# A mixture-of-experts block on one core: more expert tiles at both ends of the gate stage, and all first one-hots made on ScalarE

## Chip, core and metric

The kernel runs on one core of a Trainium2 chip. The metric is the device time of one execution in microseconds, the median of several runs.

## What is computed

One layer for a prompt of 512 tokens and 32 sample tokens (8 sequences of 4): two kinds of attention, an output projection, and then the part that matters here, a PEER layer (128 x 128 experts of one neuron each, 8 retrieval heads, the best 16 each), with a last normalization behind it. For a block of tokens `xt` of 1024 values:

```python
q = (xt @ w_query).reshape(T, 8, 256)
s1 = einsum("thc,nc->thn", q[..., :128], k1)
s2 = einsum("thc,nc->thn", q[..., 128:], k2)
v1, i1 = top_k(s1, 16); v2, i2 = top_k(s2, 16)
cand = v1[..., :, None] + v2[..., None, :]
cidx = i1[..., :, None] * 128 + i2[..., None, :]
top, pos = top_k(cand.reshape(T, 8, 256), 16)
eidx = take_along_axis(cidx.reshape(T, 8, 256), pos, -1)
g = softmax(top)
hid = einsum("thkd,td->thk", u_tab[eidx], xt)
out = einsum("thk,thkd->td", g * gelu(hid), v_tab[eidx])
```

All data is float32.

## The kernel before

The 512 + 32 tokens lie in five token tiles. Tiles 1 to 3 (384 prompt tokens) are computed densely: all 16,384 experts in 128 expert tiles of 128, with a matrix of gates that is zero where an expert was not chosen. Tile 0 and the sample tokens go sparsely: for each of the 128 slots of a token the row of the table is gathered from memory (32 rounds of five gathers, each of 128 rows of 1024) and VectorE forms the dot product.

Float32 products are made of three passes over split operands: the rounded high part (`uhi`, `vhi`, made by ScalarE) and the rest (`ulo`, `vlo`, made by GpSimd in the query stage and by VectorE later). The stages that matter:

- **Query stage** (`@block` functions from L1382). In a loop of eight turns: a head's queries and scores, VectorE's top-16 selection, and four expert tiles of hidden values, `hidden_product` (L1322, 24 matmuls of 384 columns). ScalarE makes a tile's Gelu and issues its store to memory (`hidden_gelu`, L1333), then rounds the tile after the next (`u_split_hi`, L1313). Behind the loop `QX` = 8 more expert tiles run (L1510, L1476, L1433) while VectorE ends the last head and the softmax of the gates, with ScalarE's Exp at the last of them (L1478). The SP queue loads tiles four ahead, and then spreads the sample's indices and gates (L1399 to L1406).
- **Gate stage** (L1677 to L1898). Each stage's block ends with a barrier of all engines. Three transposes (L1679) bring the indices and gates of a token into columns (`slotT`). Then six turns, each of `GTI` = 14 expert tiles interleaved with 16 groups of four tokens. For a group, four products of one-hot matrices (`oh` for the first index, `og` for the second, weighted by the gate) give the gates of four tokens over all experts in PSUM. ScalarE evicts them into `gst` (L1862), and after eight groups issues a store of 2 MB (`gate_matrix`, L1853). VectorE makes the low part of every tile (L1785), `og` of every group, `oh` of every second one by a comparison with a row of numbers (L1762, L1763), and the dots of the sparse tokens (L1772). ScalarE makes the other `oh` as four Abs of a difference and one Relu (`first_one_hot`, L1830). Four one-hot buffers stand in a ring, and they are made two groups ahead. POOL issues the gathers and cuts `slotT` into chunks of 32 tokens. Behind the turns `GX` = 4 expert tiles run, then ten dots, the Gelu of the sparse hidden values (L1879), and `coef`.
- **Value stage** (L1903 on). For each of the 128 expert tiles VectorE weighs the hidden values with the gates (`af`, L2001), ScalarE rounds `vhi` and `ahi`, VectorE makes `vlo` and `alo`, and 18 matmuls of 512 columns accumulate into PSUM. VectorE also adds the gathered value rows (L1978). SP loads value tiles one at a time, and hidden values and gates four tiles at a time (`load_gates`, L1625) into two buffers.

The order is written by hand. In a turn ScalarE does a tile's part behind every second half of a tile (L1845) and a group's part behind the half where TensorE does the group:

```python
for i in range(GTI):
    for part in range(2):
        half_tile(i, part)
        upto = N2 * (2 * i + part + 1) // (2 * GTI)
        while at < upto:
            group(at)
            at += 1
```

## Time and profile before

| | us |
|---|---|
| median of 3 runs (lowest to highest) | 1867.72 (1864.65 to 1868.74) |
| profiled execution, own time | 1864.95 |
| its span, first to last instruction | 1863.4 |
| TensorE matmuls busy | 1691.0 (91%) |
| VectorE busy | 1397.9 (75%) |
| ScalarE busy | 776.9 (42%) |
| GpSimd busy | 570.6 (31%) |
| mean transfer rate | 253 GB/s |

PE is TensorE (PEld its weight loads), DVE VectorE, ACT ScalarE, POOL GpSimd, SP the engine that only issues transfers. A busy share is an average over stages with different limits; what a stage could give is read from the waits in it. A time in brackets in a timeline is the engine's idle time before the instruction, with who ended it. Matmuls are pipelined, so their durations overlap: what one costs is read from start to start.

### The profile page before, as it was taken

To read this page: it belongs to the slowest core of one execution; us is meant where nothing else is said; L and a number is where in the kernel's file an instruction comes from. 1 tells how busy PE (TensorE), PEld (TensorE's weight loads), DVE (VectorE), ACT (ScalarE), POOL (GpSimd) and SP (SyncE) were. 2 spreads that over 40 slices of the span, in tenths; PEclk is the share of its full clock that TensorE was granted. 3 is DMA by queue.
4 is the path that set the end of the run, shared out by engine and by line. 5 is a ranking of instruction groups with operands and counts; after the bars stand their busy time and mean duration, and the time that the engine had idled before them with its cause. 6 is when DMAs were issued, how large, how long until landed. Compare 5 with 4: busy or idle time off the path is not lost. (4 is left out here: it accounts for less than half of the span.)

```text
span 1863.4 us, 30406 instructions
## 1 busy us (share of the span) xinstructions
PE 1691.0 (91%) x9914; PEld 1486.2 (80%) x9914; DVE 1397.9 (75%) x3179; ACT 776.9 (42%) x1195; POOL 570.6 (31%) x508
## 2 busy tenths in 40 slices
PE   5997898779799999779989999996899999999994
PEld 4997643449699999779989999996688888888883
DVE  3234267534389999968979888987898999999995
ACT  3222034221444433256657666663333333333333
POOL 0010280000354544433323333332433333333330
PEclk9998899899799999989999999998899999999997
DMA  3242361261343432379998998999999999999992
GB/s 112 97 174 94 121 214 46 83 232 43 116 143 111 138 115 82 124 259 350 345 376 304 366 354 332 380 338 361 363 386 387 384 384 384 384 384 389 385 385 81
DMA packets 195215, 470.82 MB, mean 253 GB/s; under 512 B 17922, under 2 KB 100482, under 8 KB 192558
## 3 DMA queue, kind: packets, MB, share of 16 engines
q1 hardware_dynamic: 124014, 240.30, 36.7%
q0 software_dynamic: 50944, 178.96, 26.0%
q10 hardware_dynamic: 20160, 50.34, 6.9%
q8 instruction: 52, 0.85, 0.2%
q14 instruction: 45, 0.37, 0.1%
HBM read 411.97 MB, written 61.32 MB: 254 GB/s over the span
## 5 line engine op out<-in xcount | busy, mean ns | idle before, releaser
L226 PE MATMUL hp<-mid_hi,uhi 128*128 128x384 f32 x1024 | 355.3, 347 | 12.0 <-issue 6.0
L227 PE MATMUL hp<-mid_lo,uhi 128*128 128x384 f32 x1024 | 345.7, 338 | 0.0
L228 PE MATMUL hp<-mid_hi,ulo 128*128 128x384 f32 x1024 | 344.4, 336 | 0.0
L226 PE MATMUL va<-vhi,ahi 128*128 128x512 f32 x768 | 299.6, 390 | 22.6 <-DVE alo L2010 22.6
L227 PE MATMUL va<-vlo,ahi 128*128 128x512 f32 x768 | 299.4, 390 | 0.0
L228 PE MATMUL va<-vhi,alo 128*128 128x512 f32 x768 | 299.2, 390 | 0.0
L2026 POOL DMA_INDIRECT gathered<-in_v_experts,idx_row x160 | 186.5, 1166 | 323.9 <-DVEq L1981 289.7
L1719 POOL DMA_INDIRECT gathered<-in_u_rows,idx_row x160 | 169.2, 1058 | 312.9 <-DVE hrow L1772 228.0
L226 PEld LDWEIGHTS hp<-mid_hi,uhi 128*128 128x128 f32 x1024 | 193.8, 189 | 17.3 <-DVE ulo L1785 8.6
L1316 ACT ACTIVATE uhi<-uw 128x1024 fp32r<-128x1024 f32 x128 | 135.7, 1060 | 151.9 <-PE hp L228 101.9
L1955 ACT ACTIVATE vhi<-vw 128x1024 fp32r<-128x1024 f32 x128 | 134.8, 1053 | 144.3 <-DMA vw<-in_v_experts 144.1
L228 PEld LDWEIGHTS hp<-mid_hi,ulo 128*128 128x128 f32 x1024 | 193.6, 189 | 0.0
L227 PEld LDWEIGHTS hp<-mid_lo,uhi 128*128 128x128 f32 x1024 | 193.6, 189 | 0.0
L226 PEld LDWEIGHTS va<-vhi,ahi 128*128 128x128 f32 x768 | 144.5, 188 | 53.0 <-issue 22.9
L1772 DVE CUSTOM_DVE_ANT_0 gathered<-gathered,x2p 128x1024 f32<-128x1024 f32 x150 | 178.7, 1213 | 8.7 <-DMA gathered<-in_u_rows,idx_row 6.4
L228 PEld LDWEIGHTS va<-vhi,alo 128*128 128x128 f32 x768 | 144.6, 188 | 30.1
L227 PEld LDWEIGHTS va<-vlo,ahi 128*128 128x128 f32 x768 | 144.6, 188 | 30.0
L2005 DVE TENSOR_TENSOR vlo<-vw,vhi 128x1024 fp32r<-128x1024 f32 x128 | 156.1, 1219 | 14.6 <-ACT vhi L1955 14.3
L1978 DVE SCALAR_TENSOR_TENSOR acc<-gathered,crow,acc 128x1024 f32<-128x1024 f32 x128 | 164.0, 1282 | 3.7 <-DMA gathered<-in_v_experts,idx_row 3.7
L1320 POOL TENSOR_TENSOR ulo<-uw,uhi 128x1024 fp32r<-128x1024 f32 x42 | 106.2, 2529 | 130.5 <-ACT uhi L1316 130.4
L1785 DVE TENSOR_TENSOR ulo<-uw,uhi 128x1024 fp32r<-128x1024 f32 x86 | 105.1, 1222 | 54.1 <-ACT uhi L1316 53.4
L1957 ACT ACTIVATE ahi<-af 128x384 fp32r<-128x384 f32 x128 | 66.9, 522 | 184.6 <-DVE af L2001 184.5
(328 smaller groups left out, 3306.2 us busy)
## 6 DMA issues: line engine op xcount, KB each, us to landing
uw<-in_u_experts SPq DMA_DIRECT2D x128, 512.0 KB, 6.7
vw<-in_v_experts SPq DMA_DIRECT2D x128, 512.0 KB, 10.6
hidden_values<-gelu_out ACTq DMA_DIRECT2D x128, 192.0 KB, 5.4
gate_matrix<-gst ACTq DMA_DIRECT2D x12, 2048.0 KB, 12.7
mid_hi<-hidden_values SPq DMA_DIRECT2D x32, 768.0 KB, 11.9
mid_lo<-gate_matrix SPq DMA_DIRECT2D x32, 768.0 KB, 16.6
pw<-in_w_qk SPq DMA_DIRECT2D x16, 512.0 KB, 3.5
qw<-in_w_query SPq DMA_DIRECT2D x16, 512.0 KB, 5.0
```

What stands on the lines that cost most here:

```text
L226: nc.tensor.matmul(out, a_hi, b_hi, start=first, stop=False)
L227: nc.tensor.matmul(out, a_hi, b_lo, start=False, stop=False)
L228: return nc.tensor.matmul(out, a_lo, b_hi, start=False, stop=last)
L1316: nc.scalar.activation(uhi[:, i], uw[:, r], ACT.Copy).then_inc(u_hi, 1)
L1320: nc.gpsimd.tensor_tensor(ulo[:, i], uw[:, r], uhi[:, i].bitcast(F32), ALU.subtract).then_inc(u_lo, 1)
L1719: nc.gpsimd.indirect_dma_start(gb[:, b], None, u_table, bass.IndirectOffsetOnAxis(ap=idx_row[:, slot, b:b + 1], axis=0)).then_inc(gathered ...
L1772: nc.vector.tensor_tensor_reduce(out=gb[:, b], in0=gb[:, b], in1=x2p[:, b // SG], scale=1.0, scalar=0.0, op0=ALU.mult, op1=ALU.add, accum_ ...
L1785: nc.vector.tensor_tensor(ulo[:, i], uw[:, r], uhi[:, i].bitcast(F32), ALU.subtract).then_inc(u_lo, 1)
L1955: nc.scalar.activation(vhi[:, c], vw[:, c], ACT.Copy).then_inc(s["vhi"], 1)
L1978: nc.vector.scalar_tensor_tensor(acc0[:], gb[:, c], crow[:, q, c:c + 1], acc0[:], ALU.mult, ALU.add).then_inc(s["s0"], 1)
L2005: nc.vector.tensor_tensor(vlo[:, c], vw[:, c], vhi[:, c].bitcast(F32), ALU.subtract).then_inc(s["vlo"], 1)
L2026: nc.gpsimd.indirect_dma_start(gb[:, b], None, v_table, bass.IndirectOffsetOnAxis(ap=idx_row[:, slot, b:b + 1], axis=0)).then_inc(gathered ...
```

## The change

`QX` goes from 8 to 16 and `GX` from 4 to 8, so `GTI` falls from 14 to 12. What stood at the start of the gate stage moves into the query stage's last tiles: the transposes and their copies behind tiles 12 to 14, the copy of `x2p` to PSUM at tiles 0 and 1, VectorE's building of the tables, and the first round of gathers on POOL. Exp stands at tile 11. On the SP queue the loads of tiles 15 to 19 go behind the transfers of the gates. What stood at the start of the value stage moves to the last eight tiles of the gate stage: the first four value tiles are rounded and split, the first round of value rows is gathered, the first gates are loaded and the first four tiles weighed. The ten last dots are dealt out between the low parts. Gates are weighed in place (`hd`, no `af`), so a buffer of `load_gates` is free only when `alo` is made. The second pair of buffers lies where the expert tiles lay (`uw`). ScalarE makes `oh` for all groups.

```diff
-        QX, GX = 8, 4
+        QX, GX = 16, 8
+        MIX = 11
...
-                for e in range(QX + UR):
+                for e in range(MIX + UR):
...
+                for e in range(MIX + UR, QX + UR):
+                    u_fetch(sp, RT * NH + e, e % UR)
...
+                    if e == QX - 3:
+                        for b in range(3):
+                            fetch_u_row(pool, 0, 0, b)
...
+                    if e == QX - 2:
+                        for b in range(3, ROW):
+                            fetch_u_row(pool, 0, 0, b)
...
+                    hidden_gelu(act, RT * NH + e, e % 2)
+                    if e < 2:
+                        act.wait_ge(s["sev"], 2 * NH + 1)
+                        act.wait_ge(x2r_spread, 16 * SG)
+                        nc.scalar.activation(x2p[:, e], x2r[:, e], ACT.Copy).then_inc(gs["x2p"], 1)
+                    if e == MIX:
                         act.wait_ge(s["exin"], 1)
                         nc.scalar.activation(GG[:], GG[:], ACT.Exp).then_inc(s["ex"], 1)
-                    hidden_gelu(act, RT * NH + e, e % 2)
+                    if MIX < e <= MIX + 3:
+                        act.wait_ge(gs["tr"], e - MIX)
+                        nc.scalar.activation(slotT[:, e - MIX - 1], tp, ACT.Copy).then_inc(gs["trev"], 1)
...
+                    if MIX < e <= MIX + 3:
+                        i = e - MIX - 1
+                        pe.wait_ge(s["ev"], 2 * NH + 1)
+                        pe.wait_ge(table_prep, (2, 2, 3)[i])
+                        if i:
+                            pe.wait_ge(gs["trev"], i)
+                        for t in range(TDT):
+                            last = nc.tensor.transpose(tp[:, t * P:(t + 1) * P], (I1, I2, GG)[i][:, t + 1], ident[:])
+                        last.then_inc(gs["tr"], 1)
...
+                dve.wait_ge(table_prep, 3)
+                nc.vector.tensor_copy(sgate[:, :, 0:SG], GG[:, 0].rearrange("p (g k) -> p g k", k=SG))
+                dve.wait_ge(table_spread, 16 * 2 * SG)
+                nc.vector.tensor_copy(sgate[:, :, SG:], spread_gate[:])
+                nc.vector.tensor_copy(eidx[:, 0:SR, SG:], spread_idx[:]).then_inc(gs["tab"], 1)
+                dve.wait_ge(gs["tab"], 1)
+                nc.vector.tensor_copy(idx_row[:], eidx[:, 0:RJ]).then_inc(gs["idx"], RJ)
+                dve.sem_inc(gs["dot"], ROW)
...
+        def weigh(dve, c, par):
+            nc.vector.tensor_tensor(hd[par][:, c].rearrange("p (c t) -> p c t", c=NCH),
+                                    hd[par][:, c].rearrange("p (c t) -> p c t", c=NCH), gt[par][:, :, c], ALU.mult).then_inc(xs["a"], 1)
+
+        def round_v(act, c):
+            nc.scalar.activation(vhi[:, c], vw[:, c], ACT.Copy).then_inc(xs["vhi"], 1)
+
+        def rest_of_v(dve, m, c):
+            dve.wait_ge(xs["vhi"], m + 1)
+            nc.vector.tensor_tensor(vlo[:, c], vw[:, c], vhi[:, c].bitcast(F32), ALU.subtract).then_inc(xs["vlo"], 1)
+
+        def round_a(act, m, c, par):
+            act.wait_ge(xs["a"], m + 1)
+            nc.scalar.activation(ahi[:, c], hd[par][:, c], ACT.Copy).then_inc(xs["ahi"], 1)
+
+        def rest_of_a(dve, m, c, par):
+            dve.wait_ge(xs["ahi"], m + 1)
+            nc.vector.tensor_tensor(alo[:, c], hd[par][:, c], ahi[:, c].bitcast(F32), ALU.subtract).then_inc(xs["alo"], 1)
...
                         pe.wait_ge(s["oh"], j * N2 + i + 1)
-                        if i % 2:
-                            pe.wait_ge(s["first"], j * N2 // 2 + i // 2 + 1 + GR // 2)
+                        pe.wait_ge(s["first"], j * N2 + i + 1 + GR)
                         pe.wait_ge(s["ev"], j * N2 + i + 1)
...
-                for b in range(ROW):
-                    fetch_row(0, 0, b)
                 over_turns(pool, turn)
                 for b in range(ROW):
-                    fetch_row(SR - 1, 1, b)
+                    fetch_u_row(pool, SR - 1, 1, b)
+                for b in range(ROW):
+                    fetch_v_row(pool, 0, 0, b)
...
-                        if i % 2 == 0:
-                            nc.vector.tensor_scalar(oh[:, i % RING, k], iota[:], col(1), None, ALU.is_equal)
                         last = nc.vector.tensor_scalar(og[:, i % RING, k], iota[:], col(0), col(2), ALU.is_equal, ALU.mult)
...
+                last_dots = [(q, b) for q in range(2) for b in range(ROW)]
                 for e in range(GX - 2):
                     split_lo(NK - GX + e + 2, e % 2, (e + 2) % UR)
-                for q in range(2):
-                    for b in range(ROW):
+                    for q, b in last_dots[3 * e:3 * e + 3]:
                         dve.wait_ge(gathered[b], 16 * (SR - 2 + q) + 16)
                         nc.vector.tensor_tensor_reduce(out=gb[:, b], in0=gb[:, b], in1=x2p[:, b // SG], scale=1.0, scalar=0.0,
                                                        op0=ALU.mult, op1=ALU.add,
                                                        accum_out=hid[:, SR - 2 + q, b:b + 1]).then_inc(s["dot"], 1)
+                    if e == GX - 4:
+                        dve.wait_ge(s["dot"], SR * ROW + ROW)
+                        nc.vector.tensor_copy(idx_row[:, 0:BR], eidx[:, 0:BR]).then_inc(xs["idx"], BR)
+                        dve.sem_inc(xs["fetched"], ROW)
+                        dve.wait_ge(stored[1], 16 * (NI + 1))
+                        for c in range(GT):
+                            rest_of_v(dve, c, c)
                 dve.wait_ge(s["act"], 1)
                 nc.vector.tensor_tensor(coef[:], hid[:], sgate[:], ALU.mult)
+                dve.wait_ge(gld[0], 32)
+                for c in range(GT):
+                    weigh(dve, c, 0)
+                for c in range(GT):
+                    rest_of_a(dve, c, c, 0)
...
-                        if i % 2 and i + 2 < N2:
+                        if i + 2 < N2:
                             first_one_hot(j, i + 2)
-                        elif i % 2 and not last:
+                        elif not last:
                             first_one_hot(j + 1, i + 2 - N2)
...
+                    if 1 <= e <= GT:
+                        act.wait_ge(stored[0], 16 * (NI + 1))
+                        act.wait_ge(vld[e - 1], 16)
+                        round_v(act, e - 1)
+                    if e == GX - 3:
+                        act.wait_ge(s["dot"], SR * ROW + ROW)
+                        act.wait_ge(s["hrow"], NI)
+                        nc.scalar.activation(hid[:], hid[:], ACT.Gelu).then_inc(s["act"], 1)
+                    if e == GX - 2:
+                        act.wait_ge(s["mm"], NI * N2 + RING)
+                        for c in range(GT):
+                            round_a(act, c, c, 0)
...
+                for e in range(UR, GX):
+                    u_fetch(sp, NK - GX + e, e % UR)
                 for u in range(2):
                     sp.wait_ge(stored[u], 16 * (NI + 1))
                 for i in range(2):
                     sp.wait_ge(ge_stored[i], 8 * 2 * GT + 16)
-                sp.wait_ge(h_mm, NK + 2)
-                for g in range(2):
-                    load_gates(sp, g, g)
-        pick.close()
-        query.close()
+                sp.wait_ge(s["cut"], 2 * NI)
+                load_gates(sp, 0, 0)
+                for i in range(GT):
+                    sp.wait_ge(xs["vlo"], i + 1)
+                    sp.dma_start(vw[:, i], A["v_experts"][GT + i]).then_inc(vld[i], 16)
+                sp.wait_ge(u_lo, NK + 2)
+                load_gates(sp, 1, 1)
...
-                            sp.wait_ge(s["a"], (g - 1) * GT)
+                            sp.wait_ge(s["alo"], (g - 1) * GT)
```

POOL, at the end of the query stage and the start of the gate stage, before (`ulo` is the low part of an expert tile, `gathered` the buffer of gathered rows):

```order
L1320 TENSOR_TENSOR ulo<-uw,uhi 128x1024 x12
L1350 UNCONDITIONAL_BRANCH
L1702 UNCONDITIONAL_BRANCH
L1711 COPY chunkT<-slotT 128x96
L1719 DMA gathered<-in_u_rows,idx_row 128x1024 x5
```

and now:

```order
L1324 TENSOR_TENSOR ulo<-uw,uhi 128x1024 x18
L1369 DMA gathered<-in_u_rows,idx_row 128x1024 x3
L1324 TENSOR_TENSOR ulo<-uw,uhi 128x1024
L1369 DMA gathered<-in_u_rows,idx_row 128x1024 x2
L1324 TENSOR_TENSOR ulo<-uw,uhi 128x1024
L1372 UNCONDITIONAL_BRANCH
L1786 UNCONDITIONAL_BRANCH
L1795 COPY chunkT<-slotT 128x96
```

The five gathers of the first round stand ahead of the last two low parts and of the end of the block (the two branches).

ScalarE inside a turn, before (`gst` the evicted gates, `oh` the first one-hots, `uhi` the rounded tile):

```order
L1840 ACTIVATE oh<-oh 128x512
L1334 REGISTER_ALU
L1335 ISA
L1336 ACTIVATE gelu_out<-hp 128x384
L1338 ISA
L1338 DMA hidden_values<-gelu_out 128x384
L1314 ISA
L1316 ACTIVATE uhi<-uw 128x1024
L1861 REGISTER_ALU
L1862 ACTIVATE gst<-ggp 128x4x128
L1334 REGISTER_ALU
L1336 ACTIVATE gelu_out<-hp 128x384
```

and now:

```order
L1911 ACTIVATE oh<-oh 128x512
L1338 REGISTER_ALU
L1339 ISA
L1340 ACTIVATE gelu_out<-hp 128x384
L1342 ISA
L1342 DMA hidden_values<-gelu_out 128x384
L1318 ISA
L1320 ACTIVATE uhi<-uw 128x1024
L1933 REGISTER_ALU
L1934 ACTIVATE gst<-ggp 128x4x128
L1907 ACTIVATE oh<-iota,chunkT 128x128 x4
L1911 ACTIVATE oh<-oh 128x512
```

Every `gst` is now followed by four Abs and a Relu on `oh`; before, every second one.

ScalarE in a turn now, from the issue of a gate store on:

```order
L1925 DMA gate_matrix<-gst 128x4096
L1933 REGISTER_ALU
L1934 ACTIVATE gst<-ggp 128x4x128
L1907 ACTIVATE oh<-iota,chunkT 128x128 x4
L1911 ACTIVATE oh<-oh 128x512
L1338 REGISTER_ALU
L1340 ACTIVATE gelu_out<-hp 128x384
L1342 ISA
L1342 DMA hidden_values<-gelu_out 128x384
L1320 ACTIVATE uhi<-uw 128x1024
```

One group (eviction and one-hots) follows the store, then a tile with its own hidden store. Behind these rows stand a group, a tile, a group, and then the Gelu that writes the buffer this hidden store reads; at a turn's end it is the same with a tile first.

## Rows read from the trace of the kernel before

**Rows 1.** Stages: us; busy of PE, PEld, DVE, ACT, POOL; clock; DMA share; GB/s

```profile
746.70:780.00 33.30, 32.65 (x187) 32.01 (x185) 30.69 (x104) 10.70 (x16) 20.53 (x8) 1.00 0.47 172
780.00:806.60 26.60, 2.36 (x10) 1.59 (x10) 17.82 (x68) 5.83 (x7) 2.34 (x1) 0.58 0.12 42
806.60:1273.90 467.30, 448.28 (x2787) 438.13 (x2785) 407.33 (x986) 310.21 (x506) 164.56 (x163) 0.99 0.94 351
1273.90:1290.80 16.90, 16.87 (x99) 16.55 (x97) 12.60 (x22) 4.88 (x7) 6.37 (x7) 1.00 0.95 346
1290.80:1313.30 22.50, 0.00 (x0) 0.00 (x0) 12.25 (x20) 4.30 (x6) 8.04 (x9) 0.55 1.03 339
1313.30:1837.50 524.20, 524.15 (x2304) 433.55 (x2304) 474.29 (x579) 191.28 (x254) 181.69 (x155) 1.00 1.02 371
```

**Rows 2.** Groups by line, the six gate turns: count | busy, mean ns | idle before, releasers

```profile
L226 PE MATMUL hp<-mid_hi,uhi 128*128 128x384 f32 x673 | 236.5, 351 | 11.4 <-issue 6.0 <-DVE ulo L1785 5.2
...
L1785 DVE TENSOR_TENSOR ulo<-uw,uhi 128x1024 fp32r<-128x1024 f32 x83 | 101.4, 1222 | 49.9 <-ACT uhi L1316 49.2 <-DVE hid L1780 0.2
...
L1836 ACT ACTIVATE oh<-iota,chunkT 128x128 f32<-128x128 f32 x192 | 59.6, 388 | 0.0
...
L1336 ACT ACTIVATE gelu_out<-hp 128x384 f32<-128x384 f32 x84 | 40.8, 486 | 89.9 <-PE hp L228 61.2 <-DMA hidden_values<-gelu_out 28.4
L1840 ACT ACTIVATE oh<-oh 128x512 f32<-128x512 f32 x48 | 30.4, 633 | 1.5
```

**Rows 3.** Timeline of PE: start, us; one group of the gate stage

```profile
1263.68 1.05 PE L1693 MATMUL ggp<-og,oh 128*128 128x128 f32 x8
1264.49 0.42 PE L226 MATMUL hp<-mid_hi,uhi 128*128 128x384 f32 x1
```

**Rows 4.** Timeline of PE at seam 1: first transposes, first product

```profile
803.08 0.87 PE L1683 MATMUL ggp<-ident,I 128*128 128x128 f32 x3 [23.11 <-PEq L1350]
...
806.58 0.67 PE L226 MATMUL hp<-mid_hi,uhi 128*128 128x384 f32 x1
```

**Rows 5.** Timeline at seam 1: ACT, SP's queue, POOL

```profile
797.03 0.74 ACT L1480 ACTIVATE GG<-GG 128x640 f32<-128x640 f32 x1 [14.60 <-DVE GG L1600]
...
799.94 2.45 SPq L1406 DMA_DIRECT2D spread_gate<-GG  x4
...
781.20 2.34 POOL L1320 TENSOR_TENSOR ulo<-uw,uhi 128x1024 fp32r<-128x1024 f32 x1 [1.68 <-ACT uhi L1316]
...
811.07 0.95 POOL L1719 DMA_INDIRECT gathered<-in_u_rows,idx_row  x1 [0.30 <-issue]
```

**Rows 6.** The page's DMA issues: count, KB each, us to landing

```profile
uw<-in_u_experts SPq DMA_DIRECT2D x128, 512.0 KB, 6.7
...
hidden_values<-gelu_out ACTq DMA_DIRECT2D x128, 192.0 KB, 5.4
...
mid_lo<-gate_matrix SPq DMA_DIRECT2D x32, 768.0 KB, 16.6
```

**Rows 7.** Timeline of ACT, one stretch of a turn without a free moment

```profile
873.55 1.14 ACT L1862 ACTIVATE gst<-ggp 128x512 f32<-128x512 f32 x1
874.48 1.24 ACT L1836 ACTIVATE oh<-iota,chunkT 128x128 f32<-128x128 f32 x4
...
876.28 0.47 ACT L1336 ACTIVATE gelu_out<-hp 128x384 f32<-128x384 f32 x1
...
878.32 1.11 ACT L1862 ACTIVATE gst<-ggp 128x512 f32<-128x512 f32 x1
```

**Rows 8.** Timeline of ACT: two gate stores and the Gelu held by a store

```profile
855.32 0.71 ACTq L1853 DMA_DIRECT2D gate_matrix<-gst  x1
...
871.50 0.49 ACT L1336 ACTIVATE gelu_out<-hp 128x384 f32<-128x384 f32 x1 [2.37 <-DMA hidden_values<-gelu_out]
...
884.95 0.34 ACTq L1853 DMA_DIRECT2D gate_matrix<-gst  x1
...
900.12 0.49 ACT L1336 ACTIVATE gelu_out<-hp 128x384 f32<-128x384 f32 x1 [3.10 <-DMA hidden_values<-gelu_out]
```

185 lines of the change are left out of this document (85 added, 100 removed).

## Prediction

> **What bounds the kernel now.** I read first the busy times stage by stage, then who made TensorE wait, then the in-order work of each engine that feeds it. In the stage table [rows 1] TensorE works through the eight expert tiles at the end of the query stage in 33.3 us, 4.16 us a tile. Then come 26.6 us with almost nothing on it, 467.3 us of six gate turns, four more tiles in 16.9 us, 22.5 us with nothing, and the value stage: 524.2 us, TensorE busy in all of it. So the value stage can give nothing, and the change can only win in the two holes (49 us together) and in the turns.
>
> A turn lasts 467.3 / 6 = 77.9 us. TensorE needs 14 tiles of 4.16 us and 16 groups of one-hot products. A group takes 1264.49 - 1263.68 = 0.81 us [rows 3], so a turn's own work is 58.2 + 13.0 = 71.2 us, and 6.7 us a turn are waits and slower work. One wait is 6.0 us that nothing in the profile explains and 5.2 us wait on VectorE's low parts [rows 2]; the hidden product starts late, once at the loop's return, else by parts of a us. The turns are thus bound by TensorE, with VectorE close behind it.
>
> **Seam 1, query to gate.** Removed: the hole of 26.6 us. In it run the softmax tail, the table's transfers, the three transposes and the start of the gathers. Added before the barrier:
> - eight tiles moved here, 8 x 4.16 = +33.3 us;
> - three sets of transposes between tiles, each 0.87 us [rows 4] at the half clock that the hole leaves (0.58 in its mean, [rows 1]), 0.5 at full clock: +1.5 us;
> - a late tile. The SP queue now loads tile 15 of the seam only behind the transfers of the gates. Exp ran at 797.03 [rows 5]; now it stands on ScalarE behind the rounding and Gelu of tile 11, whose product ends at 746.7 + 12 x 4.16 = 796.6, and so ends near 800.6, 2.8 us later than 797.77. The gate transfers, issued from 799.94 for 2.45 us [rows 5], move to about 802.7 to 805.2. The tile is issued at 805.2, just when ScalarE wants to round it. Loads take 6.7 us at the median [rows 6]; half the engines' time is free here, so I take 4. Rounding, about 1 us, the greater part of ScalarE's 2.04 for a tile [rows 7], and the low part on GpSimd, 2.34 [rows 5], end near 813, and TensorE wants the tile at 810.7: +2.3 us;
> - the end of the block. GpSimd does the last low part, but two row gathers stand ahead of it, 0.95 + 0.30 = 1.25 us each [rows 5]; three others stand before the low part of the tile ahead. Counted along its queue, 3 gathers, a low part, 2 gathers and the last low part end about 7.3 us behind the last product. The barrier takes 0.7: the SP queue had ended at 799.94 + 2.45 = 802.39 [rows 5] and TensorE began at 803.08 [rows 4]. TensorE stands 8.0 us. Bounds: 4.2 (rounding, low part and barrier alone) and 11.
>
> Sum 45.1 us for 26.6: **+18.5 us**. Exp, the building of the tables, the x2p and slotT copies lie beside the products: ScalarE is taken for 2.04 us [rows 7] of each 4.16. If that cover goes, they cost their 3 to 4 us.
>
> **The turns.** Each turn loses 2 tiles and keeps its 16 groups: TensorE needs 12 x 4.16 + 13.0 = 62.9 us. VectorE drops two low parts and all 32 one-hot comparisons of a turn. ScalarE takes them: every group now has four Abs and a Relu where every second one had. The order is one queue, so its costs are start-to-start times [rows 7]: an eviction 874.48 - 873.55 = 0.93, a one-hot set 876.28 - 874.48 = 1.80, a tile (Gelu, its store's issue, the rounding) 878.32 - 876.28 = 2.04 us. Before: 14 x 2.04 + 16 x 0.93 + 8 x 1.80 = 57.8 us. Now: 12 x 2.04 + 16 x 0.93 + 16 x 1.80 = **68.2 us**. ScalarE becomes the longest queue, 5 us above TensorE.
>
> To this comes a wait of ScalarE itself. Twice a turn a 2 MB gate store is issued on its DMA queue, and a hidden store behind it lands late: the Gelu that reuses its buffer began 871.50 - 855.32 = 16.2 and 900.12 - 884.95 = 15.2 us after such a gate store [rows 8], having waited 2.37 and 3.10 us; in all 28.4 us of the turns go there [rows 2]. Until now ScalarE had time to spare, so nothing was lost. In the new order (third excerpt of the order, and the same at a turn's end) ScalarE needs 12.2 us of its own from the gate store to the Gelu that waits: three groups and two tiles (12.2). It will stand there 15.7 - 12.2 = 3.5 us, twice: +7.0. A turn is then **75.2 us**.
>
> Six turns are 451.2. The last gate store's wait falls behind the turns, -3.5; filling and draining the queue at both ends, -3.0 (less than two one-hot sets); the 6.0 us of TensorE at the loop's return stay, but that turn's store wait hides in it, +2.5. So 447.2 instead of 467.3: **-20.1 us**.
>
> Other bounds of a turn: at 351 GB/s and 0.94 of the DMA engines [rows 1] a turn moved 27.3 MB. Less two tiles and their stores (0.72 MB each) it is 25.9 MB, and with the engines always busy (373 GB/s) 69.5 us. So a turn lies between 69.5 and, with half of before's 6.7 us of loss on top of 75.2, about 78.4.
>
> The Trainium skill (ScalarE: Activation LUTs, Rules for kernel authors) says to use VectorE and not ScalarE for relu and the like, and to budget some 0.3 us for each ACTIVATE plus 0.83 ns an element. By that a one-hot set would be 2.4 us, 9 us more a turn, and the sum would end slower by about 50 us. The trace has 1.80 us start to start, and that decides.
>
> **Seam 2, gate to value.** Before: 16.9 + 22.5 = 39.4 us. Now eight tiles, 33.3 us. The last dots, the fifth row's gather, the first four value tiles' high and low parts and the first gates lie beside them. VectorE has 6 low parts, 10 dots and 4 value low parts for it, 20 of 1.22 us [rows 2] or a little less, and 8 short ones: under 29 us. What stays is the end: Gelu and issue of the last hidden store, 1.0 us, its landing, 5.4 us at the median [rows 6], for which ScalarE waits before the barrier, 0.7 for the barrier, and 0.9 for a low part late behind a dot that waits for its gather: 8.0 us (bounds 4 and 12). 41.3 for 39.4: **+1.9 us**.
>
> **Value stage.** TensorE needs its 524.2 us and has its first four tiles ready: 0. The gates are now weighed in place, so their buffer is free some 3 us later, after the low part of the group before; they took 16.6 us to land [rows 6], in a cycle of 16.4 us a group. The lead of a group with which the stage starts covers that.
>
> **Sum.** +18.5 - 20.1 + 1.9 = +0.3 us on the profiled execution's 1864.95, so 1865.3. The median of the runs lies 2.8 us above that execution; that gives 1868.1, and I forecast **1868 us**. What a measurement can tell from no change is 0.2%, 3.7 us.
>
> **Rivals.**
> (a) *TensorE stays the bound.* The waits on stores shrink because the DMA engines have fewer tiles a turn, and ScalarE catches up. For it: ScalarE's 68.2 us is only 5 above TensorE's. A turn keeps today's 6.7 us of loss: 62.9 + 6.7 = 69.6, six are 417.6, -49.7; with both seams -29.3: 1838 us on the runs' scale. Against it: the order shows no free stretch on ScalarE for a wait of 3 us.
> (b) *Slower: ScalarE's lag reaches TensorE.* The low part of tile m+2 needs ScalarE's rounding, which waits in line behind one-hot sets; TensorE has one tile and one or two groups, 5 to 6 us, until it needs it, and 2.04 + 1.22 us of that are spent. Once ScalarE lags over 2 us, both stall in turn. At 3.2 us a turn, the upper bound of 78.4, it is +19: 1887 us. For it: VectorE's low parts already cost TensorE 5.2 us [rows 2].
> (c) *Slower: gates land late in the value stage.* It decides if landing passes 17 us. At 18 us each of 15 pairs of groups takes 1.6 us more, 24 us, less the lead of 16: +8, 1876 us.
> (d) *Short activations do not overlap.* 4 x 0.388 + 0.633 [rows 2] = 2.19 us a set, 6.2 us a turn, +37: 1905. [...]
> (e) *The change doesn't do what it says*: a barrier or the late tile keeps the holes as long as they were, so 33.3 + 1.5 us are added at seam 1, not 18.5: 1884 us.
>
> **Numbers.** Forecast case, a turn of 73.5 to 76.5 us: 0.53, which alone spans 1857 to 1876; (a) and what lies between 0.24; (b) 0.12; (c) 0.05; (d) 0.02; (e) 0.04. Half of the bounds' width at the seams is in the first case, so 0.17 of it is faster by over 0.2%, 0.20 within, 0.16 slower. Faster 0.41, same 0.20, slower 0.39. The range takes half of (a) and of (b): 1842 to 1886.
>
> **What would show it.** Seam 1: TensorE stands 6 to 10 us at the barrier, and one low part late near the 15th tile. The turns: gate stores of a turn's end 75 us apart; on ScalarE almost no wait for TensorE (61.2 us now [rows 2]) but still some 35 us for hidden stores; TensorE's waits are for ScalarE's one-hots, a releaser that is missing now. Seam 2: about 7 us between last hidden and first value product. Wrong it would be if turns are under 72 us with ScalarE idle for TensorE, or if value products wait for low parts in mid stage.

## The result, and the profile after

The changed kernel takes 1903.88 us at the median of four runs (1902.51 to 1907.4), the kernel before 1868.23 on the same chip (1864.65 to 1873.72). The ratio is 1.0197, its 95% interval 1.018 to 1.0214: **slower by 1.8 to 2.1%**, 36 us. The forecast was 1868, its range 1842 to 1886. The profiled execution took 1902.88 us, its span is 1901.3. In the experiments below, one execution of seam2_order ran at a lower clock, 1998.87 us, and its median leaves it out.

First the stages of the changed kernel, in the columns and with the cuts of [rows 1]: seam 1 behind the eighth tile, the turns, the products of seam 2, the wait at its end, the value stage, the end.

```profile
785.40:838.10 52.70, 38.30 (x202) 36.80 (x200) 26.19 (x68) 17.60 (x24) 27.72 (x15) 0.89 0.48 164
838.10:1296.40 458.30, 408.28 (x2497) 399.42 (x2498) 356.27 (x782) 362.63 (x719) 152.66 (x157) 0.96 0.92 336
1296.40:1340.40 44.00, 37.54 (x192) 36.29 (x191) 32.56 (x51) 16.80 (x23) 17.25 (x15) 0.91 0.90 334
1340.40:1350.40 10.00, 0.03 (x1) 0.00 (x0) 0.00 (x0) 0.62 (x2) 0.15 (x1) 0.75 1.06 386
1350.40:1874.70 524.30, 524.26 (x2302) 433.90 (x2303) 472.04 (x572) 194.72 (x250) 182.70 (x156) 0.99 1.00 366
```

Seam 1 took 52.7 us where 26.6 stood, the turns 458.3 where 467.3 stood, seam 2 54.0 (44.0 and 10.0) where 39.4 stood; the value stage did not change. Neither TensorE (408 us busy of 458) nor ScalarE (363) fills the turns now. And 5.4 us were lost before any of it, in code that the change does not touch; the last copy of scores began at 737.52 us before and at 742.95 after.

From that copy on every profile below is cut into the same pieces: to the first hidden product of the turns (seam 1), to the last eviction of a gate group (turns), to the first value product (seam 2), to the end. The prediction in this scale: 42.5 us from the copy to the eighth tile's end at 780.0 before, and 45.1 behind it.

| | ahead | seam 1 | turns | seam 2 | value on | span |
|---|---|---|---|---|---|---|
| before | 737.5 | 69.1 | 467.6 | 39.2 | 550.1 | 1863.4 |
| predicted | 737.5 | 87.6 | 447.2 | 41.3 | 550.1 | 1863.7 |
| after | 742.9 | 95.4 | 458.1 | 54.0 | 550.9 | 1901.3 |
| difference to the prediction | +5.4 | +7.8 | +10.9 | +12.7 | +0.8 | +37.6 |

**The turns.** The groups of instructions there, in the columns of [rows 2]:

```profile
L226 PE MATMUL hp<-mid_hi,uhi 128*128 128x384 f32 x577 | 207.3, 359 | 16.5 <-PEq L1372 9.1 <-issue 5.1 <-DVE ulo L1850 2.3
...
L1907 ACT ACTIVATE oh<-iota,chunkT 128x128 f32<-128x128 f32 x384 | 119.0, 387 | 7.5 <-POOL chunkT L1795 7.5
...
L1777 PE MATMUL ggp<-og,oh 128*128 128x128 f32 x768 | 107.2, 284 | 42.3 <-DVE og L1828 42.3
...
L1340 ACT ACTIVATE gelu_out<-hp 128x384 f32<-128x384 f32 x72 | 34.6, 481 | 48.3 <-PE hp L228 27.5 <-DMA hidden_values<-gelu_out 20.8
```

TensorE now waits 42.3 us ahead of the one-hot products, and the releaser named is VectorE's second one-hots. In the kernel before this was 7.3 us (columns: us in total, times, longest):

```profile
PE ggp L1693 <- DVE og L1763: 7.3, 13, 1.2
```

ScalarE's queue is fuller than its busy time of 363 us says: 42 us of its idle time (37.1 and 5.0 in the waits) lie between Gelu and rounding, where it issues the store, so about 405 us are its own work. One of TensorE's waits, in time (start, us, engine, line), ScalarE first, then VectorE, then TensorE:

```profile
850.20 1.12 ACT L1934 ACTIVATE gst<-ggp 128x512 f32<-128x512 f32 x1
851.09 1.24 ACT L1907 ACTIVATE oh<-iota,chunkT 128x128 f32<-128x128 f32 x4
852.37 0.63 ACT L1911 ACTIVATE oh<-oh 128x512 f32<-128x512 f32 x1
852.90 0.47 ACT L1340 ACTIVATE gelu_out<-hp 128x384 f32<-128x384 f32 x1
...
854.00 1.06 ACT L1320 ACTIVATE uhi<-uw 128x1024 fp32r<-128x1024 f32 x1 [0.62 <-ACT gelu_out L1340]
...
855.09 1.23 DVE L1850 TENSOR_TENSOR ulo<-uw,uhi 128x1024 fp32r<-128x1024 f32 x1 [2.93 <-ACT uhi L1320]
856.24 1.11 DVE L1828 TENSOR_SCALAR og<-iota,chunkT 128x128 f32<-128x128 f32 x4
...
857.59 1.13 PE L1777 MATMUL ggp<-og,oh 128*128 128x128 f32 x8 [1.33 <-DVE og L1828]
```

The tile was finished near 851.0, half way between two groups of TensorE. ScalarE was then in an eviction and a set of one-hots, until 852.90; Gelu, the store's issue and the rounding took until 855.0. VectorE had stood 2.93 us for the rounding with its own one-hots in line behind the low part, and TensorE, 1.33 us early, waited for them. Every second group had such a set before; now every group has one.

**Seam 1.** First VectorE's softmax tail in the kernel before:

```profile
790.77 1.83 DVE L1585 TENSOR_TENSOR eq<-eq,XF 128x1280 bf16<-128x1280 bf16 x2
...
794.82 0.32 DVE L1590 TENSOR_TENSOR pk<-eq 128x160 f32<-128x160 bf16 x1
...
799.09 0.82 DVE L1612 TENSOR_TENSOR GG<-GG,sm 128x640 f32<-128x640 f32 x1
```

and in the changed kernel VectorE's tail, GpSimd, Exp and the late tile on ScalarE, SP's queue, TensorE:

```profile
796.36 6.00 DVE L1636 TENSOR_TENSOR eq<-eq,XF 128x1280 bf16<-128x1280 bf16 x2
...
804.59 2.30 DVE L1641 TENSOR_TENSOR pk<-eq 128x160 f32<-128x160 bf16 x1
...
810.84 2.75 DVE L1663 TENSOR_TENSOR GG<-GG,sm 128x640 f32<-128x640 f32 x1
...
799.13 2.42 POOL L1324 TENSOR_TENSOR ulo<-uw,uhi 128x1024 fp32r<-128x1024 f32 x1 [0.66 <-ACT uhi L1320]
...
830.90 0.95 POOL L1369 DMA_INDIRECT gathered<-in_u_rows,idx_row  x1 [0.30 <-issue]
831.87 2.35 POOL L1324 TENSOR_TENSOR ulo<-uw,uhi 128x1024 fp32r<-128x1024 f32 x1
...
808.78 0.74 ACT L1520 ACTIVATE GG<-GG 128x640 f32<-128x640 f32 x1 [2.61 <-DVE GG L1651]
...
819.81 1.06 ACT L1320 ACTIVATE uhi<-uw 128x1024 fp32r<-128x1024 f32 x1 [6.64 <-DMA uw<-in_u_experts]
...
816.07 2.00 SPq L1315 DMA_DIRECT2D uw<-in_u_experts  x4
...
809.28 0.61 PE L1561 MATMUL ggp<-ident,I 128*128 128x128 f32 x3 [2.17 <-DVE sample_idx L1656]
...
822.30 0.52 PE L1561 MATMUL ggp<-ident,GG 128*128 128x128 f32 x3 [2.26 <-ACT slotT L1523]
823.35 0.69 PE L226 MATMUL hp<-mid_hi,uhi 128*128 128x384 f32 x1 [0.53 <-POOL ulo L1324]
838.36 0.68 PE L226 MATMUL hp<-mid_hi,uhi 128*128 128x384 f32 x1 [9.07 <-PEq L1372]
```

The two products of ranks and indices took 6.00 us where they took 1.83 before, the sum behind them 2.30 for 0.32, the gates' last product 2.75 for 0.82. Exp came 65.8 us behind the last copy of scores (59.5 before), and all that follows with it: the loads behind the gates' transfers were issued at 816.07 and ScalarE stood 6.64 us for tile 15. TensorE stood 2.17 us for VectorE's indices ahead of the first transposes and 2.26 us ahead of the last; behind each its granted clock was about 0.6 (0.59 from 809.3 to 813.5, 0.61 from 822.3 to 826.5), near the level of 1.2 GHz. At the end it stood 9.07 us, though GpSimd's last low part ended at 834.22, some 4 us before the products began.

**Seam 2.** VectorE's dots and low part, ScalarE's Gelu behind the last gate store, TensorE:

```profile
1310.05 1.22 DVE L1877 CUSTOM_DVE_ANT_0 gathered<-gathered,x2p 128x1024 f32<-128x1024 f32 x1 [4.33 <-DMA gathered<-in_u_rows,idx_row]
...
1313.04 1.22 DVE L1877 CUSTOM_DVE_ANT_0 gathered<-gathered,x2p 128x1024 f32<-128x1024 f32 x1 [1.76 <-DMA gathered<-in_u_rows,idx_row]
...
1314.18 1.22 DVE L1850 TENSOR_TENSOR ulo<-uw,uhi 128x1024 fp32r<-128x1024 f32 x1
...
1312.31 0.49 ACT L1340 ACTIVATE gelu_out<-hp 128x384 f32<-128x384 f32 x1 [3.94 <-DMA hidden_values<-gelu_out]
...
1322.73 0.49 ACT L1340 ACTIVATE gelu_out<-hp 128x384 f32<-128x384 f32 x1 [7.46 <-PE hp L228]
...
1315.46 0.69 PE L226 MATMUL hp<-mid_hi,uhi 128*128 128x384 f32 x1 [5.93 <-DVE ulo L1850]
...
1350.44 0.77 PE L226 MATMUL va<-vhi,ahi 128*128 128x512 f32 x1 [10.01 <-PEq L1734]
```

Two dots waited 4.33 and 1.76 us for their rows with the low part of the fourth tile behind them. TensorE stood 5.93 us. The tile behind this wait took until 1322.7, 7.2 us instead of 4.16, at a granted clock of 0.58, so most of it at the level of 1.2 GHz and not of 2.4; the four behind it were back at 1.00:

```profile
1315.40:1322.70 7.30, 7.24 (x25) 7.24 (x26) 6.50 (x11) 0.00 (x0) 2.72 (x3) 0.58 1.03 386
1322.70:1340.30 17.60, 17.07 (x96) 16.24 (x95) 14.91 (x23) 9.15 (x14) 7.49 (x5) 1.00 0.80 276
```

At the end TensorE stood 10.01 us.

### The profile page after: what moved, and what is told of

Read it like the earlier page. It is cut to its first block and busy times, and to the rows that moved or that the text cites. A ratio compares the mean times of both kernels' runs of the same rounds, so it can differ in the third digit from the quotient of the medians.

```text
span 1901.3 us, 30382 instructions
## 1 busy us (share of the span) xinstructions
PE 1711.6 (90%) x9914; PEld 1504.1 (79%) x9914; DVE 1364.4 (72%) x2979; ACT 854.8 (45%) x1435; POOL 586.3 (31%) x516
## 5 line engine op out<-in xcount | busy, mean ns | idle before, releaser
L226 PE MATMUL hp<-mid_hi,uhi 128*128 128x384 f32 x1024 | 362.2, 354 | 24.7 <-PEq L1372 9.1
L227 PE MATMUL hp<-mid_lo,uhi 128*128 128x384 f32 x1024 | 351.9, 344 | 0.0
L228 PE MATMUL hp<-mid_hi,ulo 128*128 128x384 f32 x1024 | 350.2, 342 | 0.0
L1369 POOL DMA_INDIRECT gathered<-in_u_rows,idx_row x160 | 163.3, 1021 | 320.2 <-DVE hrow L1837 206.3
L226 PEld LDWEIGHTS hp<-mid_hi,uhi 128*128 128x128 f32 x1024 | 199.1, 194 | 29.8 <-issue 16.4
L227 PEld LDWEIGHTS hp<-mid_lo,uhi 128*128 128x128 f32 x1024 | 198.7, 194 | 0.0
L228 PEld LDWEIGHTS hp<-mid_hi,ulo 128*128 128x128 f32 x1024 | 198.3, 194 | 0.0
L1324 POOL TENSOR_TENSOR ulo<-uw,uhi 128x1024 fp32r<-128x1024 f32 x50 | 125.2, 2505 | 148.4 <-ACT uhi L1320 148.4
L1724 DVE TENSOR_TENSOR vlo<-vw,vhi 128x1024 fp32r<-128x1024 f32 x128 | 156.1, 1222 | 12.5 <-ACT vhi L1720 10.6
L1850 DVE TENSOR_TENSOR ulo<-uw,uhi 128x1024 fp32r<-128x1024 f32 x78 | 95.4, 1223 | 82.8 <-ACT uhi L1320 72.7
L1777 PE MATMUL ggp<-og,oh 128*128 128x128 f32 x768 | 107.2, 284 | 42.3 <-DVE og L1828 42.3
```

Of the source, the lines that this page charges most:

```text
L226: nc.tensor.matmul(out, a_hi, b_hi, start=first, stop=False)
L227: nc.tensor.matmul(out, a_hi, b_lo, start=False, stop=False)
L228: return nc.tensor.matmul(out, a_lo, b_hi, start=False, stop=last)
L1324: nc.gpsimd.tensor_tensor(ulo[:, i], uw[:, r], uhi[:, i].bitcast(F32), ALU.subtract).then_inc(u_lo, 1)
L1369: nc.gpsimd.indirect_dma_start(gb[:, b], None, u_table, bass.IndirectOffsetOnAxis(ap=idx_row[:, slot, b:b + 1], axis=0)).then_inc(gathered ...
L1724: nc.vector.tensor_tensor(vlo[:, c], vw[:, c], vhi[:, c].bitcast(F32), ALU.subtract).then_inc(xs["vlo"], 1)
```

## Experiments

The theory after this look: the change makes chains longer, not queues. (1) In the turns a set of one-hots on ScalarE delays the rounding, VectorE's queue behind it, and TensorE. (2) In seam 1 VectorE is slowed by GpSimd's low parts, loads stand behind late transfers, and the barrier waits for gathers. (3) In seam 2 a low part stands behind dots, and the barrier waits for gathers and stores. The main rival: some engine or the transfers are simply full. All profiles in the cuts of the table above:

| run | ahead | seam 1 | turns | seam 2 | value on | median us | ratio to before |
|---|---|---|---|---|---|---|---|
| half_onehots | 743.8 | 94.6 | 444.8 | 58.1 | 550.7 | 1893.59 | 1.0148 (1.0124 to 1.0173) |
| before_all_scalar | 738.5 | 69.0 | 484.5 | 37.5 | 550.9 | 1881.97 | 1.0089 (1.0062 to 1.0116) |
| second_onehots_first | 751.0 | 95.5 | 438.2 | 54.9 | 550.1 | 1891.25 | 1.0124 (1.0093 to 1.0155) |
| round_before_gelu | 743.5 | 95.0 | 439.5 | 53.3 | 550.6 | 1886.09 | 1.0117 (1.0090 to 1.0144) |
| seam_loads_first | 742.9 | 91.3 | 455.5 | 53.5 | 551.1 | 1897.60 | 1.0173 (1.0145 to 1.0202) |
| seam_gathers_last | 746.3 | 102.4 | 455.4 | 53.0 | 551.1 | 1907.49 | 1.0217 (1.0192 to 1.0242) |
| fewer_low_parts | 744.9 | 87.7 | 456.8 | 53.9 | 550.3 | 1895.47 | 1.0154 (1.0130 to 1.0178) |
| seam2_order | 747.0 | 95.1 | 453.5 | 52.1 | 549.9 | 1902.02 | 1.0209 (1.0173 to 1.0245) |
| gathers_behind_barriers | 745.9 | 90.9 | 451.9 | 48.7 | 552.1 | 1894.11 | 1.0160 (1.0124 to 1.0195) |
| all_orders | 744.8 | 86.0 | 442.2 | 50.0 | 551.8 | 1877.98 | 1.0062 (1.0041 to 1.0084) |
| all_orders_half | 744.7 | 86.0 | 429.2 | 50.3 | 553.9 | 1867.36 | 0.9999 (0.9975 to 1.0022) |
| before_round_first | 740.0 | 69.1 | 453.6 | 38.3 | 550.0 | 1851.51 | 0.9922 (0.9897 to 0.9947) |
| half_more_bytes | 744.6 | 86.0 | 436.2 | 49.5 | 552.5 | 1871.18 | 1.0026 (1.0013 to 1.0040) |
| before_more_bytes | 739.7 | 69.0 | 450.3 | 40.1 | 549.8 | 1851.14 | 0.9910 (0.9890 to 0.9929) |
| half_late_store_wait | 745.5 | 86.1 | 429.9 | 48.7 | 553.3 | 1871.69 | 1.0014 (0.9999 to 1.0029) |
| before_both_orders | 736.5 | 69.1 | 448.4 | 37.9 | 550.0 | 1843.35 | 0.9874 (0.9853 to 0.9895) |
| half_short_dots | 744.6 | 86.0 | 412.6 | 48.3 | 552.5 | 1845.50 | 0.9882 (0.9854 to 0.9910) |
| before_orders_all_scalar | 740.1 | 69.0 | 459.0 | 39.2 | 550.2 | 1860.10 | 0.9967 (0.9952 to 0.9983) |

### Where the one-hots are made

`half_onehots`, the changed kernel with every second set on VectorE again:

```diff
+if i % 2 == 0:
+    nc.vector.tensor_scalar(oh[:, i % RING, k], iota[:], col(1), None, ALU.is_equal)
...
-if i + 2 < N2:
+if i % 2 and i + 2 < N2:
     first_one_hot(j, i + 2)
```

> The changed kernel, but every second set of first one-hots is made on VectorE again, as before the change; both seams stay filled. Theory 1 (ScalarE's queue has become part of every turn's loop: its rounding of the next tile waits behind one-hot sets of 1.8 us, VectorE's low part and the second one-hots behind it come late, and TensorE waits): ScalarE drops 8 x 1.8 = 14.4 us a turn, TensorE's waits for VectorE's second one-hots fall from 42.3 us to under 15, a turn falls from 76.3 to 69 to 71 us, the kernel to 1865 to 1875. Theory 2 (the turns are bound by VectorE: 12 low parts, 25 dots and 16 sets of second one-hots): VectorE gets 8 sets of first one-hots more, about 8 us a turn, and the turns stay at 76 us or grow; the kernel at 1900 or above. Theory 3 (the turns are bound by the transfers): unchanged within 1 us a turn.

The turns fell by 13.3 us, not by 32 to 44: 74.1 us each, and the kernel is at 1894 us, not 1865 to 1875. TensorE's wait for VectorE fell from 42.3 to 25.9 us, not under 15. So ScalarE's load is part of the chain and not the whole of it. Seam 2 grew by 4 us, so less of it reached the time.

`before_all_scalar`, the kernel before with this one part of the change (the same edit the other way round):

> The kernel before with one thing of the change alone: the first one-hots of all groups on ScalarE, seams as before (8 and 4 tiles, 14 a turn). My sum of ScalarE's queue gives 14 x 2.04 + 16 x 0.93 + 16 x 1.80 = 72.2 us a turn, TensorE 71.2. Theory 1 (the loop through ScalarE, VectorE and TensorE costs above either queue): a turn grows from 77.9 to about 84 us, the kernel to 1895 to 1910. Theory 2 (one-hots on VectorE cost more than those on ScalarE): the turns get shorter, the kernel is at or below 1868.

The turns grew by 16.9 us (80.8 a turn, less than the 84 expected), the kernel by 0.9%, to 1882 us where 1895 to 1910 was expected. TensorE's waits for low parts grew from 5.2 to 18.1 us. Taken alone, this part of the change costs time in either kernel.

### The two orders of the turns

`second_onehots_first`:

```diff
-split_lo(G0 + GTI * j + i + 2, i % 2, slot(half, i + 2))
 while built < N2 * (i + 1) // GTI + AHEAD:
     ...
+split_lo(G0 + GTI * j + i + 2, i % 2, slot(half, i + 2))
```

> The changed kernel, with one order turned round on VectorE in the turns: the second one-hots that belong to a tile's step are built before the low part of the tile two ahead, not behind it. Theory 1, first half (TensorE waits because second one-hots stand on VectorE behind a low part that waits for ScalarE's late rounding): TensorE's waits for second one-hots fall from 42.3 us to under 15, those for low parts grow a little as each is up to 2.1 us later, a turn falls by 3 to 5 us, the kernel to 1875 to 1888. If the waits only move from the one-hots to the low parts or to ScalarE's first one-hots, the turns stay within 1 us: then ScalarE's own queue is the bound and the order on VectorE is not.

`round_before_gelu`:

```diff
-hidden_gelu(act, m, i % 2)
 u_split_hi(act, m + 2, i % 2, slot(half, i + 2))
+hidden_gelu(act, m, i % 2)
```

> The changed kernel, with one order turned round on ScalarE in the turns and in the eight tiles behind them: the tile two ahead is rounded before the Gelu and its store, so that the rounding does not wait for a hidden store's landing (20.8 us in the turns, 3.9 behind them) nor for Gelu and issue, 1.0 us. Theory 1: low parts and the second one-hots behind them come 1 us earlier and TensorE's 42.3 us of waits fall by 12 x 1.0 a turn at most, so by half or more; a turn falls by 2 to 5 us, seam 2 by 3, the kernel to 1872 to 1890. If ScalarE's queue alone is the bound: no change in the turns, the kernel within 4 us of 1904.

TensorE's waits in the turns of the first (columns: us in total, times, longest):

```profile
PE hp L226 <- DVE ulo L1850: 26.1, 26, 8.6
...
PE ggp L1777 <- DVE og L1828: 3.7, 4, 1.6
```

and of the second:

```profile
PE ggp L1777 <- DVE og L1828: 30.9, 19, 2.9
```

Each order alone takes 19 to 20 us out of the turns, 3.2 a turn, within what was expected, with every instruction as before. The waits for second one-hots went from 42.3 to 3.7 us in the one, where part of them came back as waits for low parts, and only to 30.9 in the other, where half or more was expected to go. This shows that the turns were bound by the chain from ScalarE's rounding over VectorE's queue to TensorE. The first kernel's median (1891, where 1875 to 1888 was expected) moved less than its turns; its profile lost 8 us more ahead of seam 1.

### Seam 1

`seam_loads_first`:

```diff
-for e in range(MIX + UR):
+for e in range(MIX + UR + 2):
     u_fetch(sp, RT * NH + e, e % UR)
...
+u_fetch(sp, RT * NH + MIX + UR + 2, (MIX + UR + 2) % UR)
 sp.wait_ge(table_prep, 3)
```

> The changed kernel; in seam 1 SP loads tiles 15 and 16 ahead of the transfers of the indices, tile 17 ahead of those of the gates, and 18 and 19 behind them, where it loaded 15 to 19 behind all of them. Theory A (the late tile of seam 1 is the load that stands behind the table's transfers, and these are late because Exp is): ScalarE's wait of 6.6 us for that load goes, TensorE's waits of 2.3 and 0.5 us at the third transposes and the tile behind them too, and the half clock that follows; the first product of the turns comes 3 to 7 us earlier after the last scores, the kernel at 1897 to 1901. Rival: the end of the seam is set by the table itself (Exp, gates, slotT, gathers), which are no earlier: then the first product moves by less than 1.5 us.

Seam 1 fell by 4.1 us, in the range, and ScalarE's wait for a load is gone, with TensorE's waits of 2.26 and 0.53 us: theory A holds. The 2.2 us ahead of the first transposes stay.

`fewer_low_parts`, in which most of six low parts is left out:

```diff
-u_split_lo(pool, RT * NH + e + 2, e % 2, (e + 2) % UR)
+nc.gpsimd.tensor_tensor(ulo[:, e % 2, 0, 0:16], ...)    # for 8 <= e <= 13
```

> The changed kernel; for six tiles of seam 1 (10 to 15) GpSimd computes the low part of 16 of the 1024 columns only, so most of these low parts are left out. Theory B (VectorE's softmax tail runs slowly because GpSimd's low parts run beside it: the product of the ranks with the indices took 6.0 us for 1.8, the gates' last product 2.75 for 0.82): without them these instructions take 1.8, 0.3 and 0.8 us as before the change, Exp starts about 59.5 us after the last scores' copy as it did before, not 65.8, and the gates' transfers start 8 us earlier, and with them the load behind them, so that ScalarE's wait of 6.6 us for tile 15 is under 1 us. The kernel at 1893 to 1900. Rival (VectorE's tail is slow by its own state or by the transfers): the durations stay at 6.0, 2.3 and 2.75 us.

```profile
798.17 1.83 DVE L1641 TENSOR_TENSOR eq<-eq,XF 128x1280 bf16<-128x1280 bf16 x2
...
802.24 0.33 DVE L1646 TENSOR_TENSOR pk<-eq 128x160 f32<-128x160 bf16 x1
...
809.27 0.83 DVE L1668 TENSOR_TENSOR GG<-GG,sm 128x640 f32<-128x640 f32 x1
```

VectorE's three instructions are back at 1.83, 0.33 and 0.83 us without GpSimd's low parts beside them. This shows the cause. The SBUF page of the Trainium skill (SBUF — State Buffer, SBUF: two separate sides) says that VectorE, when an instruction reads two inputs from SBUF, and GpSimd share a pair of ports, which one of them locks for a whole instruction; the trace agrees, each stretched instruction being 1.9 to 2.1 us longer, somewhat less than a low part's 2.4. It shows a little more: in the query stage of the changed kernel an instruction with one input, `ab<-ab` (L1623), took 2.45 us beside a low part, at 648.18, where it takes 0.20 in the kernel before. Exp itself came 62.3 us behind the last scores and not 59.5: VectorE had its input ready at 804.4, but Exp stands behind tile 11 on ScalarE, which was done with it at 805.5, and behind a table load of 1.28 us. That is 2.8 us later than before, as the prediction had it. And ScalarE still waited 4.4 us for a load, which the expectation had under 1. Seam 1 took 87.7 us, and 87.6 was predicted. TensorE's products take 34.6 us of it (34.8 in the sum), its wait for the late tile 1.8 (2.3), its stand at the end 9.0 (8.0). So the prediction's sum is close for a seam in which the stretching does not happen.

`seam_gathers_last` puts the five gathers behind the last low part, `gathers_behind_barriers` puts these and the five of the value rows behind the barriers:

```diff
-if e == QX - 3:
-    for b in range(3):
-        fetch_u_row(pool, 0, 0, b)
-if e == QX - 2:
...
+for b in range(ROW):
+    fetch_u_row(pool, 0, 0, b)    # behind the loop, or behind the barrier
```

> The changed kernel; in seam 1 GpSimd fetches the five rows of the first gather behind its last low part instead of three ahead of the last but one and two ahead of the last. Theory A (TensorE stands at the barrier for GpSimd's queue, two gathers and the low part behind them): the low part ends about 2.4 us earlier, but the barrier now waits for the issue of five gathers, 6.3 us, unless they end it: if the barrier waits for GpSimd's queue, TensorE's 9.1 us grow to 10 to 12. If the wait is set by something else (the hidden stores, SP), 9.1 stays within 1 us. A gain of over 2 us would speak for neither.

> The changed kernel; the five gathers that GpSimd issues before the barrier of seam 1, and the five of the value rows before that of seam 2, are issued behind these barriers, as before the change. Theory D (a barrier behind gathers waits until they have landed: it came 5.9 us behind the last gather's issue where two stood ahead of the last low part, and 5.5 us where all five stood behind it): seam 1's barrier comes 0.7 us behind the last low part, and TensorE stands 5 instead of 9.1 us; at seam 2 TensorE stands 7 instead of 10 us if the gathers set it, 9.5 to 10 if the hidden stores do. The first dots of both stages are later, which cost nothing before the change. The kernel at 1895 to 1900. Rival (the barrier itself costs 3 us or more in this kernel): TensorE still stands 8 to 9 us in seam 1.

With all gathers behind the last low part TensorE stood 15.9 us, 4 more than the 12 us expected at most: the barrier came 5.5 us behind the end of the last gather's issue. With none ahead of the barrier:

```profile
PE hp L226 <- PEq L1372: 4.5, 1, 4.5
```

Seam 1 fell by 4.5 us and seam 2 by 5.3. So the barrier waits for gathers that are under way; the same gathers behind it cost the turns nothing (451.9 us, even 6.2 less, which is not explained), and from the value stage on the kernel is 1.2 us longer. With gathers ahead of the barrier GpSimd's next instruction came 5.0 to 6.2 us behind the end of the last gather's issue, in eight profiles; with none it came 0.5 us behind the last low part. That the barrier waits until the gathers have landed fits this, but no row shows their landing there. The last hidden store is not the cause: with all gathers last it had landed at 836.2 us, 12 us before the turns began.

### Seam 2

`seam2_order`:

```diff
-for q, b in last_dots[3 * e:3 * e + 3]:
+for q, b in last_dots[(0, 1, 1, 4, 7, 10, 10)[e]:(0, 1, 1, 4, 7, 10, 10)[e + 1]]:
```

and in ScalarE's loop of these tiles the rounding ahead of Gelu.

> The changed kernel; in the eight tiles behind the turns VectorE does one dot behind the first low part, none behind the second and three behind each of the next three (it was three behind each of the first three, one behind the fourth), and ScalarE rounds before Gelu and its store there. Theory C (seam 2 is 54 us and not 41 because a low part stands behind dots that wait for their gathers, 5.9 us at TensorE, after which its granted clock is lower): TensorE's wait falls to under 2 us, the clock of the stretch rises, last group to first value product takes 44 to 49 us, the kernel 1894 to 1899. Rival (the hidden stores behind the last 2 MB gate store set it, whatever the order): Gelu still waits and TensorE loses 4 us or more.

The expectation failed. Seam 2 fell by 1.9 us only: TensorE still waited 8.7 us for low parts, 6.8 at the most. The clock of the products moved from 0.91 to 0.92 only. The medians do not tell it from the changed kernel. The trace shows why:

```profile
1328.16 4.63 DVE L1724 TENSOR_TENSOR vlo<-vw,vhi 128x1024 fp32r<-128x1024 f32 x4
1332.70 1.22 DVE L1850 TENSOR_TENSOR ulo<-uw,uhi 128x1024 fp32r<-128x1024 f32 x1
...
1333.98 0.69 PE L226 MATMUL hp<-mid_hi,uhi 128*128 128x384 f32 x1 [6.78 <-DVE ulo L1850]
```

The wait at the fourth tile fell from 5.9 to 1.8 us, so that one was due to the dots ahead of its low part. But a new wait came at the last tile. Its rounding was done at 1323.8, and its low part stood on VectorE behind the last dots, now later, and behind the four value tiles' low parts. No run puts these behind it.

### All mended, and the kernel before with the same orders

`all_orders` joins second_onehots_first, round_before_gelu, seam_loads_first, gathers_behind_barriers and seam2_order; `all_orders_half` adds half_onehots. `before_round_first` is the kernel before with the rounding ahead of Gelu in its turns.

> The changed kernel with all orders altered at once that the single runs speak for: in the turns ScalarE rounds before Gelu and VectorE builds second one-hots before the low part; tiles 15 to 17 are loaded ahead of the table's transfers; gathers behind both barriers; the order of seam 2. If the savings add up (turns -20 to -28 us from 458, seam 1 -8, seam 2 -3 to -6), it comes to 1862 to 1874, level with the kernel before. If the two orders of the turns save the same wait, it is 1872 to 1880.

> The run all_orders with every second set of first one-hots on VectorE again. Theory 1 (ScalarE's queue is what the turns wait for, orders or not): turns shorter by 5 us or more in all than in all_orders. Rival (with the orders mended the place of the one-hots is worth nothing, VectorE being as full as ScalarE): within 3 us of it, or slower.

> The kernel before, with one order turned round: ScalarE rounds the tile two ahead before Gelu and its store in the turns. If TensorE's work and the loop through ScalarE bind its turns alike (71.2 us of own work in 77.9), it gains too: 467 us of turns fall by 5 to 15, the kernel at 1852 to 1862. If TensorE alone binds there, ScalarE having 61 us of waits for TensorE, it stays within 4 us of 1866: then this order matters only since the change.

The seams added up (seam 1 86.0, 9.4 less than in the changed kernel), the two orders of the turns did not: 442.2 together, 438.2 and 439.5 alone, with the kernel at 1878 us, in the range that was given for orders that save the same wait. Why the two together take more than either alone is open. One-hots back on VectorE again took 13 us from the turns. All mended, the changed kernel is level with the kernel before, and no more; its seam 2 still has a wait of 7.0 us for the last tile's low part. The kernel before gains 14 us by the one order: there too TensorE was held by that chain, and the rival "TensorE alone" fell.

So why does a kernel with 12 fewer tiles in its turns not win? The mended turns moved 363 GB/s with the DMA engines 0.97 busy, so the next theory (E) was that the transfers bind them. Both runs issue a store of 192 KB more for each tile:

```diff
 u_fetch(sp, G0 + GTI * j + i + UR, slot(half, i))
+sp.dma_start(spare_dram[G0 + GTI * j + i], x2hi[:, 0, P:SEQ].bitcast(F32)).then_inc(spare_done, 16)
```

> The run all_orders_half with more bytes and nothing else: behind each tile's load in the turns, SP also issues a store of 192 KB from a buffer that nobody writes to a tensor of its own that nobody reads (12 a turn, 2.36 MB). Theory E (with the orders mended the turns are bound by the transfers, 71.5 us at 363 GB/s): a turn grows by 2.36 MB / 363 GB/s = 6.5 us, 39 us in all, the kernel to 1900 to 1910. Rival (bound by the loop through the engines; the transfers' share is high but has slack): under 2 us a turn, the kernel at 1867 to 1880.

> The run before_round_first with the same stores, 14 a turn, 2.75 MB. Its turns take 75.6 us at 361 GB/s; TensorE's own work there is 71.2. Theory E: 7.6 us a turn more, 46 in all, the kernel at 1893 to 1900: then the tiles that the change takes from the turns are worth only their bytes there. Rival (TensorE binds these turns, with 4 us of slack in the transfers): 3 us a turn or less, the kernel under 1872.

The turns of all_orders_half, of half_more_bytes and of before_more_bytes, in the columns of the stage table:

```profile
830.70:1259.90 429.20, 402.78 (x2503) 393.48 (x2504) 392.71 (x976) 287.65 (x479) 163.68 (x162) 0.98 0.97 363
```

```profile
830.60:1266.80 436.20, 410.24 (x2504) 400.35 (x2505) 393.00 (x976) 287.59 (x480) 163.45 (x162) 0.96 1.01 390
```

```profile
808.70:1259.00 450.30, 441.29 (x2788) 438.02 (x2787) 407.30 (x986) 306.99 (x506) 162.96 (x163) 0.99 1.02 400
```

They move 390 and 400 GB/s in 1.2 us a turn more and in no more time at all (before_round_first, the same without the stores, has 362 GB/s at a share of 0.96). **Theory E fell**: a share of 0.97 was not a full one. Fullest in the first row beside TensorE is VectorE, 392.7 us of 429.2, with TensorE waiting 19.3 us for its low parts. Of the 36.5 us in which VectorE is idle, 20.8 are waits for gathered rows. So theory G: `half_short_dots` shortens two of five dots, which leaves out part of the sample rows' hidden values:

```diff
+n = 64 if b % 2 else D
-nc.vector.tensor_tensor_reduce(out=gb[:, b], ...
+nc.vector.tensor_tensor_reduce(out=gb[:, b, :n], ...
```

> The run all_orders_half, where VectorE multiplies and sums only 64 of the 1024 columns in two of every five dots of the turns (so part of the sample rows' hidden values is left out). Theory E fell: more bytes cost the turns 1 us each at most. Theory G (with the orders mended VectorE is what binds the turns of the changed kernel: 393 us busy of 429, TensorE waiting 19 us for its low parts): ten dots a turn drop from 1.15 to about 0.2 us, VectorE's 65.5 us a turn to 56, and TensorE with 12 tiles a turn binds: 66 to 68 us a turn instead of 71.5, the kernel 20 to 30 us lower, 1838 to 1848. Rival (TensorE and its wait for low parts behind ScalarE's rounding bind, VectorE's own time does not): under 1 us a turn, the kernel at 1860 or above.

```profile
830.60:1243.20 412.60, 398.95 (x2503) 395.01 (x2504) 335.00 (x976) 287.42 (x479) 154.13 (x163) 0.98 0.99 378
```

The turns fell to 412.6 us, 68.8 each (66 to 68 was expected), the kernel to 1845.5, as theory G has it: VectorE's work was the bound, and with less of it TensorE is busy 399 us of 413.

Three more runs fill the picture: `before_both_orders` (both orders in the kernel before), `before_orders_all_scalar` (and all first one-hots on ScalarE), and `half_late_store_wait`, in which the wait for the last hidden stores goes to the value stage:

```diff
-for i in range(2):
-    act.wait_ge(ge_stored[i], 8 * NK + 16)
...
+for i in range(2):
+    sp.wait_ge(ge_stored[i], 8 * NK + 16)    # SP, value stage
```

> The run before_round_first with the second order too: VectorE builds one-hots before the low part. Theory E: its turns are at the transfers' floor of 361 GB/s already, so nothing more comes: within 3 us of 1851.5. Rival (the loop through the engines still binds): another 3 to 8 us less, 1844 to 1848. If low parts come too late by this order (they wait up to 2 us for one-hots), it is slower, 1855 or above.

> The run before_both_orders with the first one-hots of all groups on ScalarE. With late orders this cost the kernel before 17 us in its turns, and the changed kernel with its orders mended 13. If one-hots of 1.8 us in ScalarE's queue delay its rounding and evictions whatever the orders are: 8 to 16 us slower than 1843.4, so 1851 to 1859. If TensorE's 84 tiles bind these turns and VectorE's relief is worth as much as ScalarE's load costs: within 3 us of 1843.

> The run all_orders_half with the wait for the last two hidden stores moved from ScalarE's end of the gate stage to the head of SP's queue in the value stage. Theory F (what is left of seam 2's wait at its barrier is the landing of the last hidden store): TensorE's 4.5 us between last hidden and first value product fall to 1.5 or less, the kernel 3 us lower, 1862 to 1866. Rival (the barrier or VectorE's last low parts set it): unchanged.

```profile
805.60:1254.00 448.40, 442.32 (x2793) 440.21 (x2792) 409.32 (x990) 306.44 (x506) 165.81 (x164) 0.99 0.97 367
```

In before_both_orders TensorE is busy 99% of the turns: here it is the bound. The turns fell by 5.2 us more, which theory E had excluded, the kernel to **1843.35 us, 0.9874 of before (0.9853 to 0.9895), the fastest version that does all the work**. One-hots on ScalarE still cost these turns 10.6 us and the kernel 17, a little more than expected. With the late wait for the stores TensorE stands 1.5 us at the last barrier instead of 4.5, as expected, but seam 2 is only 1.6 us shorter and the kernel is at 1871.7 us where 1862 to 1866 was expected: no gain is shown.

## Why the prediction was wrong

Two steps of the prediction failed. It took moved work to cost nothing because it lies "beside the products"; and it took a turn to be as long as its longest queue and that queue's waits for stores. In their place the runs showed work in chains from engine to engine: 7.8 us too little in seam 1, 10.9 in the turns and 12.7 in seam 2. The other 5.4 us stand ahead of all this.

**Ahead of seam 1** (0 predicted, +5.4). The query stage's code is the same. From the first to the last copy of scores within the view (505.07 to 737.52 before, 507.23 to 742.95 after) it took 232.45 us before and 235.72 after; the rest had come earlier. One sum of the candidates there took 3.03 us beside a low part where it takes 0.88, so the same collision is at work. It is no novelty of the change. The trace of the kernel before has it in this stage, where it could have been read before the forecast:

```profile
646.90 2.37 DVE L1575 SCALAR_TENSOR_TENSOR rank<-abf 128x80 bf16<-128x80 f32 x1
...
788.38 0.38 DVE L1575 SCALAR_TENSOR_TENSOR rank<-abf 128x80 bf16<-128x80 f32 x1
```

Which instructions are hit differs between the two traces, and up to the last copy of scores VectorE's take 4.2 us more in all in the changed kernel. All kernels built on the change were at 742.9 to 751.0 at this point, those built on before at 736.5 to 740.1. Why the phases fall so is open.

**Seam 1** (45.1 predicted, 52.7). The step that failed is "the building of the tables, the x2p and slotT copies lie beside the products": it does, but beside GpSimd's low parts it is stretched, 8 us up to the gates. Exp was forecast 2.8 us later than before and came 6.3 later, counted from the last scores. In TensorE's time: waits for tables and tiles 5.6 us where the late tile alone had 2.3 (and loading it early gave back 4.1), products 38.3 us for 34.8, most of this at the lower clock behind these waits, and the end 9.1 for 8.0. The end was near by luck: the last low part ended 4.9 us behind the last product, not 7.3, and the barrier took 4.1 us and not 0.7, waiting for gathers.

**The turns** (447.2 predicted, 458.1). The forecast had 75.2 us a turn and it was 76.3. A set of one-hots takes 1.81 us (851.09 to 852.90), so the trace's price held and rival (d) fell. By the figures of the Trainium skill (ScalarE: Activation LUTs, Rules for kernel authors) a set would be 2.4 us, an estimate; the trace does not agree with it. But "ScalarE becomes the longest queue" did not decide the length: its own work of about 405 us is near the 409 of the sum, and it still waited 27.5 us for TensorE. Its waits for stores were 20.8 us, not 42. The length came from the chain of rival (b), ScalarE's rounding, VectorE, TensorE, with one link that (b) did not have: the second one-hots behind the low part. So the size of a turn came out near by luck, by a store wait put too high and a chain left out; and that an order takes 19 us with no work changed is nothing that an account by queues can give. The terms for both ends, -4.0 us together, did not show. The other bound of a turn, 69.5 us for transfers at 373 GB/s, does not hold either: the turns of before_more_bytes moved 400 GB/s.

**Seam 2** (41.3 predicted, 54.0). The term "0.9 for a low part late behind a dot that waits for its gather" was 5.9, and the lower clock behind it 3.1 more. VectorE's work was summed (under 29 us) and found to fit, but not its order. The wait at the end, 7.1 in the sum, was 10.0: without the gathers 6.4. The 1.7 us that are left are open.

**Value stage** (0 predicted): right, 524.3 us for 524.2; rival (c) fell. **Rival (e)**, holes as long as they were, fell too, but seam 1 came to lie half way to it: +26.3 us, where the forecast had 18.5 and the rival 34.8.

**What decides it.** Compare before_both_orders with all_orders_half: same orders, same place of the one-hots. Twelve tiles fewer save the turns 19.2 us, 1.6 a tile and not 4.16, because VectorE keeps its 25 dots and 16 groups a turn and becomes the bound. In the seams the eight cost 16.9 us and the four 12.4. Even mended, the filling loses 10 us there. The two profiles lie 22.1 us apart: 8.2 more are lost ahead of seam 1 and 3.8 from the value stage on, and these are not explained. The prediction never asked what VectorE's queue is worth when TensorE's shrinks; it was "close behind" in its own words.

## What to carry to other kernels

Two queues that each have slack can still bind through a chain: before adding work to an engine, look for what it releases next and for what stands behind that on the next engine; the order that releases another engine first (rounding before Gelu) was worth more here than all the filling. Work moved into a hole pays only as far as the engines that feed the emptied stretch have slack too. And cover is not free where one engine's instructions hold up another's, as GpSimd's low parts did VectorE's here, or where a barrier waits for transfers under way.

## What was not expected of the hardware

- Beside a low part of GpSimd (2.4 us) single instructions of VectorE took about 2 us longer: two products together 6.00 us for 1.83, a sum 2.30 for 0.32, a product 2.75 for 0.82. They ran at 1.83, 0.33 and 0.83 when most of the low parts was left out.
- Behind a barrier with indirect gathers ahead of it GpSimd went on 5.0 to 6.2 us after the last one's issue had ended (eight profiles); TensorE stood 9.1 us with two gathers ahead of the last low part, 15.9 with five behind it, 4.5 with none.
- DMA engines shown as 0.96 and 0.97 busy at 362 and 363 GB/s took 9 to 10% more bytes, at 400 and 390 GB/s, in 3 us less of 454 and 7 us more of 429.
